# Weights of the attention heads' steps in the walk that interleaves two strands of a hybrid decoder's prompt mixer

## What is computed

```
sc = index_scores(iqb, iwb, ik, key_pos[None, :] <= qpos[:, None])
vals, idx = lax.top_k(sc, n_sel)          # n_sel = 256
...
return sparse_attend(qb, k_sel, v_sel, jnp.isfinite(vals))
```

```
sa = jnp.einsum('bhvk,bhk->bhv', S, at)
S = S * dt[:, :, None, :] + sa[..., None] * bt[:, :, None, :] + vt[..., None] * kt[:, :, None, :]
return S, jnp.einsum('bhvk,bhk->bhv', S, rt)
```

## Time and profile before

| what | value |
|---|---|
| median of 3 runs | 6515.59 us (6501.82 to 6523.53) |
| span of the profiled execution | 6596.6 us, one execution; it has no other time of its own |
| PE busy | 5426.8 us (82%) |
| DVE busy | 2900.2 us (44%) |
| ACT busy | 1507.0 us (23%) |
| mean granted clock of PE | 0.842 of full speed |

### The profile page before, as it was taken

The page is one execution under the profiler, slowest core; times in us unless marked ns, Lnnn a source line. Parts: engine busy times, 40 slices in busy tenths (PEclk is TensorE's granted clock), DMA queues, the critical chain, the costliest instruction groups (busy, mean ns, idle before and its releaser), DMA issues. The chain is left out here.

```text
span 6596.6 us, 62854 instructions
## 1 busy us (share of the span) xinstructions
PE 5426.8 (82%) x22562; PEld 3271.5 (50%) x22562; DVE 2900.2 (44%) x6756; ACT 1507.0 (23%) x3002; POOL 494.9 (8%) x522
## 2 busy tenths in 40 slices
PE   6999575475788899999989976745658989999997
PEld 4444353254566466654344434433545764666543
DVE  3366554377644233330043755544775432333201
ACT  3400222155333111100033002312553321111000
POOL 3400231000000000000033003300000000000000
PEclk9999566575879999999989996655658889999998
DMA  4231431200000331122132323311100023111122
GB/s 159 92 119 66 115 102 55 67 27 15 13 18 15 127 112 58 49 69 61 49 129 98 111 77 107 116 46 47 34 8 20 13 82 122 58 58 49 60 68 99
DMA packets 355053, 460.12 MB, mean 70 GB/s; under 512 B 72882, under 2 KB 258164, under 8 KB 354324
## 3 DMA queue, kind: packets, MB, share of 16 engines
q1 hardware_dynamic: 322020, 356.04, 16.6%
q0 software_dynamic: 32768, 100.70, 5.0%
HBM read 346.53 MB, written 120.25 MB: 71 GB/s over the span
## 5 line engine op out<-in xcount | busy, mean ns | idle before, releaser
L405 PE MATMUL pp<-w_in,nT 128*128 128x512 f32 x1792 | 815.6, 601 | 0.0
L3283 PE MATMUL pg<-nT,wgu 128*128 128x364 f32 (+1 forms) x2112 | 671.2, 471 | 15.7 <-DMA wgu<-in_w_up 15.7
L3283 PE MATMUL pu<-nT,wgu 128*128 128x364 f32 (+1 forms) x2112 | 665.1, 468 | 0.0
L3353 PE MATMUL pm<-w_down,hT 128*128 128x512 f32 x1408 | 610.5, 597 | 24.3 <-DMA hT<-scratch_hT 24.3
L3283 PEld LDWEIGHTS pg<-nT,wgu 128*128 128x128 f32 x2112 | 404.1, 191 | 260.9 <-issue 21.3
L3283 PEld LDWEIGHTS pu<-nT,wgu 128*128 128x128 f32 x2112 | 401.3, 190 | 242.3
L405 PEld LDWEIGHTS pp<-w_in,nT 128*128 128x128 f32 x1792 | 326.8, 191 | 388.5 <-issue 388.2
L3353 PEld LDWEIGHTS pm<-w_down,hT 128*128 128x128 f32 x1408 | 269.5, 192 | 364.8 <-issue 364.8
L3305 DVE TENSOR_SCALAR sig<-exp_neg 128x364 f32<-128x364 f32 x132 | 46.1, 349 | 681.2 <-ACT exp_neg L3294 681.2
L2517 POOL DMA_INDIRECT kv_sel<-in_cache_kv,kv_idx x256 | 247.2, 965 | 1217.8 <-DVE kv_idx L2660 995.9
L3306 DVE RECIPROCAL exp_neg<-sig 128x364 f32<-128x364 f32 x132 | 319.4, 2420 | 4.5
(11 more groups left out here) (678 smaller groups left out, 8072.6 us busy)
## 6 DMA issues: line engine op xcount, KB each, us to landing
w_in<-in_w_in SPq DMA_DIRECT2D x14, 2048.0 KB, 9.2
scratch_hT<-hT SPq DMA_DIRECT2D x44, 544.0 KB, 2.7
wgu<-in_w_gate SPq DMA_DIRECT2D x44, 512.0 KB, 3.9
wgu<-in_w_up SPq DMA_DIRECT2D x44, 512.0 KB, 5.1
w_down<-in_w_down SPq DMA_DIRECT2D x22, 1024.0 KB
hT<-scratch_hT SPq DMA_DIRECT2D x16, 1408.0 KB, 7.4
x_all<-scratch_x SPq DMA_DIRECT2D x27, 512.0 KB, 7.5
a_tile<-scratch_pa SPq DMA_DIRECT2D x18, 516.0 KB
```

What stands on the lines that cost most here:

```text
L405: ins = pe.matmul(pp[u % 2][:, 0:cw], nT[:, k, t * P:(t + 1) * P], w[:, k, 0:cw], start=(k == 0), stop=(k == KT - 1))
L3283: ins = pe.matmul(bank[:, 0:cw], wb[b][:, which, k, :], nT[:, k, c0:c0 + cw], start=(k == 0), stop=(k == KT - 1))
L3353: ins = pe.matmul(pm[b][n][:, :], h[b][:, k, :], w[:, k, n * 512:(n + 1) * 512], start=(k == 0), stop=(k == FT - 1))
```

## The change

Two numbers for each pair of head steps, and with them the weight of the heads among the attention strand's stretches:

```diff
     for H in range(len(HEADS) + LAG):
         w = width(HEADS[min(H, len(HEADS) - 1)][0]) / 1024
-        costs += [2.2 * w + 0.3, 2.0 * w + 0.3]
+        costs += [0.9 * w + 0.1, 0.8 * w + 0.1]
         if H >= LAG and HEADS[H - LAG][1] == BH - 1:
             out_at[attend + 2 * H + 2] = HEADS[H - LAG][0]
```

## The result

The changed kernel takes 6604.11 us (median of four runs, 6595.78 to 6614.04) against 6508.7 for before on the same chip, a ratio of 1.014 (95% interval 1.0121 to 1.016). It is 95 us slower. The forecast was no change, with a range up to 6585.

The account below looks back on a forecast made before the run. It took no engine as full in the index, DVE as leading in counting and pick, PE in the heads. Terms 22 + 43 + 23 - 90 = -2 us a layer, -4 for two, gave 6512 us, range 6455 to 6585.

Parts of the forecast that it names:

- The heads, -90: Heads stretch: with 71 RWKV steps instead of 123 it falls to 348 us, -90 us a layer.
- the bill of idle time and low clock: Heads: PE's idle time plus time lost to low clock, 102 us before, taken as 70 us after.
- The counting, +43: Counting with recover: 97 RWKV steps at 86 us a tile make 278 us, +43 us a layer.
- if the two strands simply add: Counting, lower bound: a tile sheds 4.67 rounds of 4.08 us and takes 82.9 us.
- a chain whose levels shed nothing while the other steps shed their share: Counting, upper bound: RWKV's own chain holds the levels, only 20 of 30 steps shed; 89.2 us a tile.
- the 83 to 89 that I had named as the sign: Counting: RWKV tiles 2 and 3 stored 83 to 89 us apart would show the forecast right.
- The index, +22: Index stretch: 14 more RWKV steps at 1.6 us each, +22 us a layer.
- the pick, +23: Pick: 8 more RWKV steps, with tile 5's whole front, at the upper end, +23 us a layer.
- The sum: Mixing stage: the four stretches' terms together, -2 us a layer, -4 us for two, giving 6512 us.
- The first: Counting and index: slower, the RWKV chain doesn't shrink, 89.2 us a tile; +17 a layer, 6550 us, chance 0.20.
- The third: Counting: faster, PE's clock rises, 77.4 us a tile; -30 a layer, 6456 us, chance 0.20.
- the second rival: Heads: slower, front stalls and low clock stay, -58 instead of -90; +30 a layer, 6576 us, chance 0.15.

Follow-up runs that it names:

- e4: Changed kernel with two dummy matmuls in each attention step of counting, recover and pick: 6619.92 us, ratio 1.0055 to before.
- e2: RWKV strand alone in the mixing stage, attention strand left out: 65 to 79 us a tile, most 69 to 71.
- e3: Attention strand alone in the mixing stage, RWKV strand left out: 442 us for the stage's attention.
- e10: Kernel before with costs scaled so only the index stretch takes RWKV steps from the heads (46, 67, 18, 110): 6645.16 us against 6608.68, one run.
- e8: Kernel before with costs scaled so only the pick takes RWKV steps from the heads (32, 67, 26, 116): 6609.16 us against 6591.19, one run.
- e5: Kernel before with two dummy matmuls in each attention step of counting, recover and pick: 6564.05 us, ratio 0.9961.
- e6: Kernel before with the heads' costs 1.5 times as large, so the heads hold more RWKV steps (147): 6588.9 us, ratio 1.0002.
- e12: Kernel before with heads' costs 1.5 times as large and two dummy matmuls per attention step of counting, recover and pick: ratio 1.0062.
- e15: Kernel before with DVE taking each counting RWKV step one attention step later, plus two dummy matmuls per step: 6526.06 us, ratio 1.001.

## Why the prediction was wrong, step by step

- **The heads, -90.** Right: -98 and -97 us measured. The waits at L1808 went from 29.1 us in four places to 9.8 in two. PE's work at full clock, put at 278 us, measured 278, and the bill of idle time and low clock, put at 70, measured 60. Attention's part of the work, put at 199 us, was near too: alone the heads take 216 us with PE busy 209.22. So this term was right in its mechanism.
- **The counting, +43: the step that failed.** I bounded it by "if the two strands simply add" (82.9 us a tile) and by a chain whose levels shed nothing while the other steps shed their share (89.2), and took 86. The stretch measured 301.3/3.23 = 93.2 us for 30 steps, and tiles 2 and 3 took 94.5 and 90.2 us (91.6 and 90.2 in layer 2), not the 83 to 89 that I had named as the sign: above both bounds, +66 and +65 us. The choice of 86 rested on levels at full clock being "nearly as short as the attention's own work", so that they too would shed. Tile 2 shows where it failed: the levels took 26.9 before and 29.3 now, 2.4 us more, at a clock of 0.62 instead of 0.72, and the other steps shed 9.8 us and not 12.7 (with e4's dummies, at full clock, the levels take 22.5). Already the bound of 89.2 was too low by these two, 5.3 us. In the words of e2 and e3: the counting hides 60 to 76 us of RWKV time with 53, 67 or 97 steps in it, and the steps beyond pay nearly their 2.35 us.
- **The index, +22, and the pick, +23**, failed by the same fault. The index was priced with 1.6 us a step, by the counting's average of 1.3; e10 shows 2.2, and the changed kernel paid 33 and 42 us. The pick measured +34 and +35, and e8 and e10 show that a front costs more there than I gave it.
- **The sum.** 22 + 43 + 23 - 90 = -2 a layer was forecast; it measured 33 + 66 + 34 - 98 = +36 in layer 1 and 42 + 65 + 35 - 97 = +45 in layer 2.
- **The rivals.** The first, the RWKV chain that doesn't shrink, is what happened, at over twice its price of +17 a layer. The third did not: PE was busy 186.56 of 301 us after 136.18 of 235, and the clock went from 0.56 to 0.58 only. The rule that the Trainium skill gives in TensorE: Matmul & The Clock Gate, section "What's actually happening", that the slow clock is the default and activity releases it, pointed to the faster side; this pair of traces doesn't bear that out. With e4's dummies as further activity the clock rose to 0.86, and there the trace agrees with it. That the clock matters is shown by e4: with it raised, 33 to 38 of the 65 us are gone; but e5 gains 11 to 15 at the old density, so 18 to 27 of the 65 us are what the low clock costs more where RWKV steps stand dense.
- **The range** ended at 6585, a little past the second rival, the heads. The rival that came true was put at 6550 only, since it took the chain's bound as the worst that the counting could do. A bound built on "shed their share" was an assumption, not a row.

What stays open: why the granted clock in the heads differs between kernels with the same heads (e6 and e12) and between e15's two layers (433 and 455 us), why the index of the changed kernel takes 153 us in layer 2 where e10's, with as many RWKV steps, takes 141, and why a front costs what it does in the pick. The 18 to 27 us come from the difference of e4 and e5 and not from an experiment on the clock alone.

The best version is e5: the kernel before with two dummies a step, 0.3 to 0.4% faster in two timings on different chips.

## What to carry to other kernels

When work is moved between stretches that two strands share, ask for the price of the next step, not the average of those that stand there: measure each strand alone (e2, e3), and what a stretch hides is the sum of both less its time. If a denser or thinner arrangement hides the same, each step moved there pays in full, and so does each moved away, which here made the old weights flat to one side and bad to the other. In a dependent chain look at one repeated piece, as the level here: if it is as long as with nothing beside it, it sets the pace.

## What the runs showed of the hardware that I had not expected

- The same kernel took 6508.7 and 6510.62 us in some series and 6589 to 6609 on other chips, 1.2 to 1.5% apart, with the mixing stage alike and the difference outside it (4844 to 4856 against 4929 to 4960 us in the profiles).
- Two dummy matmuls a step raised the granted clock of the counting from 0.56 to 0.81 and made the stretch shorter, not longer (235 to 223 us), and kernels with the same instructions in the heads ran them at 0.85 and 0.82, 486 and 502 us.
- A level of the inverse, a chain of PE, ACT, PE and DVE, takes at the least 7.33 us at the clock's lower level and 4.68 at full clock, with or without counts beside it on DVE and ACT.
